# Attention of one Trainium2 core: turn the probabilities four steps behind the scores, and scale each unit's second head on GpSimd

## The reference, cut to what matters

```python
# nsa: 16 heads; two branches of causal attention (selected, window), each with a gate per head and token
# swa: 16 heads, keys of the block before and the own block, with a sink per head
# even: 8 heads, |i-j| <= 128, with a sink per head
m = jnp.maximum(jnp.max(s, axis=-1, keepdims=True), sk)
p = jnp.exp(s - m)
p = p / (jnp.sum(p, axis=-1, keepdims=True) + jnp.exp(sk - m))
out = jnp.einsum('bnhgqj,bnjhd->bnqhgd', p.astype(v.dtype), vb)
```

## Time and profile before

| what | value |
|---|---|
| median of 3 runs | 2438.16 us (2437.75 to 2439.35) |
| the profiled execution's own time | 2441.44 us |
| its span | 2439.3 us |
| PE busy | 2339.3 us, 96% of the span |
| DVE busy | 1317.7 us, 54% |
| ACT busy | 957.6 us, 39% |
| POOL busy | 318.7 us, 13% |
| mean granted TensorE clock | 0.988 of full speed |

### The profile page before, as it was taken

One profiled execution on the slowest core, in us unless ns is written; L12 is line 12 of the kernel. 1 busy time (PEld: TensorE's weight loads), 2 busy tenths in 40 slices (PEclk: granted clock), 3 DMA queues, 4 the chain that ended last, 5 costly groups with the idle time before them and its releaser, 6 DMA issues.

```text
span 2439.3 us, 30299 instructions
## 1 busy us (share of the span) xinstructions
PE 2339.3 (96%) x11616; PEld 1845.5 (76%) x11616; DVE 1317.7 (54%) x1802; ACT 957.6 (39%) x1401; POOL 318.7 (13%) x255
## 2 busy tenths in 40 slices
PE   9999999999998979999998989999999999999998
PEld 7775567888886657888887767888887757788887
DVE  6448756665545575665456765333346674433333
ACT  4327753443323363443233353322313862333222
POOL 0000003110003013111003014101112002211010
PEclk9999999999999999999999999999999999999999
DMA  5220002222222102222223112222223202222222
GB/s 183 104 70 35 2 18 86 86 103 87 103 90 94 50 36 70 102 103 87 103 86 129 70 49 73 103 89 103 102 86 112 87 1 86 87 104 86 91 104 81
DMA packets 31493, 203.79 MB, mean 84 GB/s; under 512 B 4260, under 2 KB 5288, under 8 KB 7720
## 3 DMA queue, kind: packets, MB, share of 16 engines
q1 hardware_dynamic: 30104, 199.37, 23.0%
q10 hardware_dynamic: 1296, 3.15, 0.3%
HBM read 200.41 MB, written 2.10 MB: 83 GB/s over the span
## 4 chain that ended last, share of the span: by engine, by line
PE 83%; DVE 9%; ACT 5%; issue 2%; DMA 0%; SPq 0%; ACTq 0%; POOLq 0%; POOL 0%; DVEq 0%
PE D L582 72%; PE D L698 3%; PE X L684 2%; PE D L706 2%; DVE w_lo L1649 2%; DVE xg L1683 2%; ACT prob L1313 1%; ACT w_hi L1109 1%; DVE h L1708 1%; DVE prob L1981 1%; PE X L690 1%; PE X L807 1%; ACT xg L1109 1%; DVE prob L1950 0%; ACT mid L1109 0%
## 5 line engine op out<-in xcount | busy, mean ns | idle before, releaser
L582 PE MATMUL D<-xg,w_hi 128*128 128x512 f32 x3184 | 995.6, 394 | 23.8 <-DVE xg L1683 17.3
L582 PE MATMUL D<-mid,w_hi 128*128 128x512 f32 x2308 | 716.4, 392 | 20.4 <-DVE w_lo L1649 9.4
L582 PEld LDWEIGHTS D<-xg,w_hi 128*128 128x128 f32 x3184 | 601.7, 190 | 157.1 <-DVE xg L1683 19.3
L1649 DVE TENSOR_TENSOR w_lo<-w_raw,w_hi 128x2048 fp32r<-128x2048 f32 (+2 forms) x210 | 456.8, 2176 | 362.9 <-ACT w_hi L1109 362.6
L582 PE MATMUL D<-xg,w_lo 128*128 128x512 f32 x1592 | 624.7, 392 | 0.0
L1109 ACT ACTIVATE w_hi<-w_raw 128x2048 fp32r<-128x2048 f32 (+2 forms) x210 | 355.7, 1694 | 487.4 <-PE D L582 482.3
L582 PEld LDWEIGHTS D<-mid,w_hi 128*128 128x128 f32 x2308 | 434.5, 189 | 116.4 <-issue 17.9
L582 PE MATMUL D<-mid,w_lo 128*128 128x512 f32 x1154 | 450.7, 391 | 0.0
L582 PEld LDWEIGHTS D<-xg,w_lo 128*128 128x128 f32 x1592 | 301.8, 190 | 63.9
L582 PEld LDWEIGHTS D<-mid,w_lo 128*128 128x128 f32 x1154 | 217.7, 189 | 45.4
L1708 DVE TENSOR_TENSOR h<-D,h 128x1024 f32 (+1 forms) x71 | 86.8, 1223 | 260.4 <-PE D L582 260.4
(11 more groups left out here) (280 smaller groups left out, 1747.1 us busy)
## 6 DMA issues: line engine op xcount, KB each, us to landing
w_raw<-in_weights SPq DMA_DIRECT2D x184, 1024.0 KB, 4.8
h<-in_x SPq DMA_DIRECT2D x4, 512.0 KB, 7.7
out_y<-h SPq DMA_DIRECT2D x4, 512.0 KB, 2.9
w_raw<-in_weights SPq DMA_DIRECT2D x2, 512.0 KB, 7.4
inv_cnt<-in_inv_cnt ACTq DMA_DIRECT2D x1, 1024.0 KB, 5.9
cos<-in_cos ACTq DMA_DIRECT2D x3, 256.0 KB, 4.5
sin<-in_sin ACTq DMA_DIRECT2D x3, 256.0 KB, 5.3
vec<-in_vec SPq DMA_DIRECT2D x1, 272.0 KB, 2.8
```

The lines of the kernel that those rows point to most:

```text
L582: last = nc.tensor.matmul(out, w[a], x[b], start=start and k == 0, stop=stop and k == 2)
L1649: return nc.vector.tensor_tensor(out, x, f(high), ALU.subtract)
```

## The change

`LAG` goes from 3 to 4 for nsa, swa and even, so each turn, and with it each copy to `prob_t` and each product with the values, comes one step later against the scores. The buffers of the probabilities go from four to six (`prob_6`), the pairs of columns from four to eight. The vector engine scales the first head of a unit alone; GpSimd scales the second, behind it: it waits until the first head is scaled (`normed`), multiplies with the inverse sum as an operand repeated over the row, and raises a new semaphore, `second_normed`, for which the turn waits too. In nsa GpSimd first multiplies the inverse sum by the gate. In swa and even GpSimd copies the sinks of unit s before it scales the second head of unit s-1, in one queue. To make room, `idle_x` shares its memory with `kc_all`, and the last warming products read a part of the masks that is zero.

```diff
-LAG = {"nsa": 3, "swa": 3, "even": 3, "odd": 2}
+LAG = {"nsa": 4, "swa": 4, "even": 4, "odd": 2}
...
-            [("under_prob", [P, 8, SEQ], F32), ("prob_4", [P, 4, 2, SEQ], F32)],
+            [("under_prob", [P, 4, SEQ], F32), ("prob_6", [P, 6, 2, SEQ], F32)],
...
         def pair_of(a):
-            return 2 * (a % 4)
+            return 2 * (a % 8)
...
                         pe.wait_ge(normed, a0 + n + 1)
+                        if kind != "odd":
+                            pe.wait_ge(second_normed, a0 + n + 1)
...
                 dve.wait_ge(inverted, a + 1)
-                for o in range(2):
+                for o in range(2 if kind == "odd" else 1):
                     p = probs(kind, a)[:, o, 0:w]
...
-                            if s >= 4:
-                                dve.wait_ge(turned, a - 3)
+                            if s >= 6:
+                                dve.wait_ge(turned, a - 5)
...
-                for s in range(count):
+                for s in range(count + 1):
                     if kind in SINK0 and s < count:
...
-                        if s >= 4:
-                            pool.wait_ge(turned, a - 3)
-                        nc.gpsimd.tensor_copy(prob_4[:, a % 4, :, w:w + 1],
+                        if s >= 6:
+                            pool.wait_ge(turned, a - 5)
+                        nc.gpsimd.tensor_copy(prob_6[:, a % 6, :, w:w + 1],
                                               sinks[:, head:head + 2].unsqueeze(2)).then_inc(sink_in, 1)
+                    if s >= 1:
+                        a, (t, qt, branch) = a0 + s - 1, units[s - 1]
+                        c, w = pair_of(a) + 1, len(key_blocks(kind, qt)) * P
+                        p, inv = prob_6[:, a % 6, 1, 0:w], inv_sum[:, c:c + 1]
+                        if kind == "nsa":
+                            pool.wait_ge(inverted, a + 1)
+                            link(nc.gpsimd.tensor_tensor(inv, inv, gate_of(t, 1, qt, branch), ALU.mult))
+                        pool.wait_ge(normed, a + 1)
+                        ins = nc.gpsimd.tensor_tensor(p, p, inv.to_broadcast([P, w]), ALU.mult)
+                        ins.then_inc(second_normed, 1)
...
-                if kind in SINK0:
+                if kind in LAG and kind != "odd":
                     attend(kind, l)
```

More of the change, by code:

```diff
@@ L194, in build_program @@
         mla_qn, mla_qr, mla_kn, mla_kr = (normal[x] for x in ("mla_qn", "mla_qr", "mla_kn", "mla_kr"))
-        prob_4 = normal["prob_4"]
+        prob_6 = normal["prob_6"]
         w_raw = [sb(f"w_raw{s}", [P, UNIT]) for s in range(2)]
@@ L270, in build_program @@
         masks = sb("masks", [P, 7, P], BF16)
-        idle_x = sb("idle_x", [P, 2 * P], BF16)
         ssum = sb("ssum", [P, SEQ])
@@ L283, in build_program @@
         lru_work = [gates[:, k // 4, 8 * (k % 4):8 * (k % 4) + 8] for k in range(8)]
-        kc_all = sb("kc_all", [P, NSA_GROUPS, CMP_N])
+        early = overlay([("idle_x", [P, 2 * P], BF16)], [("kc_all", [P, NSA_GROUPS, CMP_N], F32)], size=NSA_GROUPS * CMP_N * 4)
+        idle_x, kc_all = early["idle_x"], early["kc_all"]
         small = overlay([("pos_x", [P, 64 + P], F32R)], [("vc_all", [P, NSA_GROUPS, HD], F32)], size=NSA_GROUPS * HD * 4)
@@ L295, in build_program @@
         block_rstd = sb("block_rstd", [P, QT])
-        neg_max = sb("neg_max", [P, 8])
-        row_sum = sb("row_sum", [P, 8])
-        inv_sum = sb("inv_sum", [P, 8])
+        neg_max = sb("neg_max", [P, 16])
+        row_sum = sb("row_sum", [P, 16])
+        inv_sum = sb("inv_sum", [P, 16])
         lru_c = sb("lru_c", [P, 3, 8])
@@ L367, in build_program @@
         inverted = sem("inverted")
+        second_normed = sem("second_normed")
         sinks_negated = sem("sinks_negated")
@@ L501, in probs @@
         def probs(kind, a):
-            return prob[:, a % 2] if kind == "odd" else prob_4[:, a % 4]
+            return prob[:, a % 2] if kind == "odd" else prob_6[:, a % 6]
         def pair_of(a):
-            return 2 * (a % 4)
+            return 2 * (a % 8)
         def query_of(kind, t, o, qt):
@@ L613, in project, with keep_busy @@
                 last.then_inc(w_used, 1)
-            def keep_busy(n):
+            def keep_busy(n, zeros):
                 for _ in range(n):
-                    nc.tensor.matmul(X[:, 0, 0:2 * P], idle_x[:, 0:P], idle_x[:, :], start=True, stop=True)
+                    nc.tensor.matmul(X[:, 0, 0:2 * P], zeros[:, 0:P], zeros, start=True, stop=True)
             def norm_sums(norm):
@@ L671, in feed_forward @@
                                 project(u0 + n, x_mid(slot), ks=ks, ends=n == 3)
-                            keep_busy(20)
+                            keep_busy(20, masks[:, 1:3, :].rearrange("p m k -> p (m k)"))
                             continue
@@ L1091, in _ @@
             pe.wait_ge(idle_in, 1)
-            keep_busy(56)
+            keep_busy(56, idle_x[:, :])
             for l, kind in enumerate(layers):
```

## The result

The changed kernel took 2424.59 us in the median of 5 runs (2420.95 to 2431.57), against 2438.16 us (2436.85 to 2442.82) for the kernel before beside it: a ratio of 0.9946, 95% interval 0.9934 to 0.9958. The forecast was 2425.2 us.

What follows compares the result with a forecast made beforehand. TensorE, busy 96% of the span, was taken as the bound, its idle time as the gain: swa 6.6, nsa 4.7, even 2.7, together 14.0, less 1.0 lost, is 13.0 us; 2438.2 - 13.0 = 2425.2 us, range 2418 to 2436.

Steps and rivals of the forecast that it cites:

- Swa, 6.6: Gain over swa's five stretches: 0.5, 0 with the scalar engine full, 1.6 with the vector engine full, 2.4 and 2.1 us.
- Nsa, 4.7: Gain in nsa: 1.6 us where `w_lo` is made, 2.4 from five stalls, 1.0 at the end, -0.3 at the start.
- At the end ... 1.0: At nsa's end, a 0.90 us wait and what the scalar engine's copies ended would give 1.0 us.
- At the start ... -0.3: At nsa's start, one more scores before the first turn would lose 0.3 us.
- Even, 2.7: Gain of 2.7 us in even's last stretch, from 3.7 us idle before turns; none while the scalar engine is full.
- The second semaphore, -1.0: Each turn's wait for a second semaphore, not in the trace, was taken to lose 1.0 us in all.
- GpSimd's price: GpSimd's second-head multiply, estimated from its subtractions: 2.18 us for a thousand columns and 0.17 fixed; nsa's gate product 0.3 us.
- The rival in which GpSimd sets the pace: GpSimd's multiply at 4.79 us per thousand columns makes a nsa tile 20.0 us; total 2444 us, slower; chance 0.12.
- the 10 us of waiting: In nsa, the port rule would hold scales back by up to 0.6 us, 16 times, within the vector engine's idle time.
- The prediction's sign of a faster mode: On the vector engine, a 256-column scale takes 0.27 us against the maximum's 0.48, so it runs in a faster mode.
- The turn gains a step and loses 0.55 us: In swa the later turn gains a 1.66 us step and loses 0.55; over 1.1 us left exceeds the 0.79 us stall.
- the stall changes its name: Rival: scores wait for the maximum, or exponentials for sinks, leaving some 5 us gained; 2433 us, 2430 to 2438; chance 0.20.

Runs made afterwards that it cites:

- nsa_on_vector: The changed kernel with GpSimd copying sinks one step earlier and, in nsa, the vector engine scaling both heads; 2424.8 us, ratio 0.9951 to the kernel before.
- lag_only: The changed kernel with the vector engine scaling both heads again, the later turn and six buffers kept; 2434.74 us, ratio 0.9984 to the kernel before.

## Why the prediction was right

The mechanism was right: the turn that waited for the scale once a tile, and its cure by one more step. That the total came out so near has luck in it. For swa the idle time is told here between points at which TensorE has done the same number of instructions as at the borders of the earlier trace rows; the order of its work differs by a step, so these shares are good to some tenths. Windows of the kernel after, cut so: the stretches with a full scalar engine, with a full vector engine, and the steady part:

```profile
839.70:853.01 13.31, 11.57 (x103) 7.05 (x101) 9.90 (x44) 13.31 (x44) 5.38 (x14) 1.00 0.00 1
853.01:865.97 12.96, 10.55 (x94) 6.46 (x92) 12.44 (x47) 10.43 (x34) 4.49 (x12) 1.00 0.28 88
865.97:885.56 19.59, 19.15 (x171) 11.79 (x167) 16.24 (x76) 18.44 (x64) 8.27 (x24) 1.00 0.13 51
```

- **The whole.** Forecast 13.0 us, measured 13.6 and 14.7. The idle time that went is 11.0 us, or 10.4 to 11.0 at full clock. So the forecast's terms were 3 us too high before the lost 1.0, and the clock, which had no term in the sum, gave 3 back. The number was closer than its working.
- **Swa, 6.6.** Measured 16.04 - 9.17 = 6.9. Idle time before and after is 3.4 and 2.1 us in the first stretch (gain 1.3, 0.5 said; part of it is hidden by half clock, 0.88 granted), 3.2 and 1.7 with a full scalar engine (1.5, 0 said), 3.0 and 2.4 with a full vector engine (0.5, 1.6 said), 2.7 and 0.4 in the steady part (2.3, 2.4 said), 3.8 and 2.5 at the end (1.3, 2.1 said). Only the steady part was right by itself. The two stretches with a full engine were taken the wrong way round: the scalar engine stays full in its stretch and TensorE still waits less there. Why was not tried.
- **Nsa, 4.7: mis-sized,** measured 2.5. Cut in the same way, as even is too, the steady part gave 2.1 (2.4 said; all five stalls went) and the stretch where `w_lo` is made 1.7 (1.6 said). Two terms failed. "At the end ... 1.0" came to nothing: there the waits are 0.19, 0.67, 0.45 and 0.40 us, 1.71 in sum, and were 0.41, 0.90 and 0.40, also 1.71. With no scores left, TensorE has only turn and values in a step, and drains at the pace of the others. "At the start ... -0.3" was -1.3 (3.0 to 4.3 us): the scores wait 0.46 and 0.65 us for the maximum in the longer fill, and some 6 us at half clock, absent after, had hidden idle time before. The two shares were not separated.
- **Even, 2.7:** 1.6. The last stretch, to which all 2.7 were given, gave 1.0; the one with a full scalar engine gave 0.7 (0 said), the start nothing. At the end two turns of 384 columns wait 0.74 and 1.08 us. The first ends with GpSimd's multiply; the second is named after the vector engine, but GpSimd's multiply (1.20 us instead of 0.83, beside a quarter of `w_lo`) ends at 1420.16 and the scalar engine's copy of the turn before at 1420.28.
- **The second semaphore, -1.0:** no run shows this term. In the steady part of swa TensorE is busy 16.00 of 16.00 us with two waits ahead of each turn.
- **GpSimd's price.** Said 0.45, 0.73 and 1.29 us for 128, 256 and 512 columns and 0.3 for the gate's product; measured 0.40, 0.61, 1.04 and 0.19. The rival in which GpSimd sets the pace needed 4.2 us for a thousand columns and is out: it was 1.67, and even with all multiplies done twice nsa's steady part is hardly touched.
- **The shared port.** Nsa's scales were not held back in after (546 and 347 ns for 512 and 128 columns, 544 and 344 before), so the 10 us of waiting that the prediction worked out did not come, and that they would have been hidden was not put to the test. Only with the multiply doubled does it happen (785 and 627 ns). A quarter of `w_lo` was held: 862 ns in nsa against 687. The prediction's sign of a faster mode set 0.27 us from start to start against a length of 0.48; by length it is 0.35 against 0.48.
- **"The turn gains a step and loses 0.55 us".** Shown from both sides: without the step the stall grows from 0.79 to 1.26 us (0.48 to 1.08 in nsa), with it it goes. The margin by which the maximum was to be in time is 0.1 us by the prediction's own figures (3.9 against 4.0), though its rivals call it 0.2. It held in the steady part and failed where `w_lo` adds to the vector engine's step, so the rival "the stall changes its name" is true in that stretch and at the starts.
- **The offload's own worth.** The prediction gave it 1.6 us in swa and the rest as cover. With the later turn it is worth 10.4 to 11.0 less 7.9, some 3 us, by 1.5 us of idle time in nsa (after against `nsa_on_vector`) and 2.0 in swa (after against `lag_only`).

## What to carry to other kernels

One more step of distance hid a loop through three engines where each of them still had slack (2.3 of 2.7 us in the steady part of swa), and least where the vector engine was full (0.5 of 3.0); one step was right here, two were worse, so the distance should be tried on both sides. Move work to a second engine together with the step that covers its slower pace: each half alone was worth 7.9 and -5.0 us, both 10.4 to 11.0. Compare idle time by stage and the granted clock before believing a difference of a few us: a kernel with 8 us less to do at full clock looked like 4.

## What the runs showed of the hardware

The port between vector engine and GpSimd behaves as a lock on a whole instruction, in both directions. A fp32 scale of 256 columns goes from 354 to 826 ns when GpSimd's multiply starts with it (0.61 us, unchanged); a scale that starts 0.3 us ahead keeps its time, and the multiply gets longer. The Trainium skill ("SBUF — State Buffer", "Who interferes with whom") says so, and also that a two-input operation of the vector engine contends with GpSimd's reads. Here the trace agrees: a quarter of `w_lo` takes 739 ns on average against 686 before, and 978 in nsa with the doubled multiply. The masked maximum, which reads its scores from PSUM, stays at 479 ns for 256 columns beside GpSimd's multiplies, as before.

The multiply on GpSimd costs 1.67 us for a thousand columns and 0.19 fixed (0.40 and 1.04 us for 128 and 512), less than the 2.18 worked out from its subtractions; that it reads one operand repeated over the row is the likely reason, not a shown one.
